# Splitting a stage's third weight block among the normalised highs, and moving the stages' SBUF region ahead of the small tiles

## The reference

```python
def rms_norm(x, g):
    y = xf * lax.rsqrt(jnp.mean(xf * xf, axis=-1, keepdims=True) + RMS_EPS)
    return (y * g).astype(x.dtype)
u = modulate(rms_norm(h, norm2_g[l]), sh2, sc2)
h = h + g2 * (relu(u @ w1) ** 2 @ w2)
```

## Time and profile before

| | us |
|---|---|
| median of 3 runs | 2047.86 |
| the runs | 2047.71, 2047.86, 2052.12 |
| profiled execution, its time | 2051.87 |
| profiled execution, its span | 2050.1 |
| busy in the span: PE | 1994.9 |
| DVE | 960.3 |
| ACT | 682.7 |
| POOL | 914.1 |
| mean granted TensorE clock | 0.983 of full speed |

### The profile page before, as it was taken

One profiled execution on the slowest core, in us unless ns is written; L12 is line 12 of the kernel. 1 busy time (PEld: TensorE's weight loads), 2 busy tenths in 40 slices (PEclk: granted clock), 3 DMA queues, 4 the chain that ended last, 5 costly groups with the idle time before them and its releaser, 6 DMA issues. The chain is left out here.

```text
span 2050.1 us, 25693 instructions
## 1 busy us (share of the span) xinstructions
PE 1994.9 (97%) x10116; PEld 1634.1 (80%) x10116; DVE 960.3 (47%) x1471; ACT 682.7 (33%) x900; POOL 914.1 (45%) x699
## 2 busy tenths in 40 slices
PE   8998998999999999999998999999999999999998
PEld 6875787888888888888887767888888887888887
DVE  4477858583937451413233264266663453113123
ACT  4231733121212431222233354355654342122122
POOL 3323364454545524545454212444344554444444
PEclk9998999999999999999999999999999999999999
DMA  8535132443523312222222111221222222222221
GB/s 349 179 93 213 43 144 109 179 177 147 209 82 148 136 63 99 86 102 95 89 102 89 62 42 59 101 83 62 83 73 92 83 83 103 85 101 103 84 81 42
DMA packets 42783, 223.07 MB, mean 109 GB/s; under 512 B 12737, under 2 KB 13249, under 8 KB 17345
## 3 DMA queue, kind: packets, MB, share of 16 engines
q1 hardware_dynamic: 42688, 221.77, 29.5%
HBM read 217.55 MB, written 2.10 MB: 107 GB/s over the span
## 5 line engine op out<-in xcount | busy, mean ns | idle before, releaser
L970 POOL TENSOR_TENSOR wl<-raw,wh 128x512 fp32r<-128x512 f32 x611 | 833.5, 1395 | 1048.7 <-ACT wh L528 976.3
L1076 PE MATMUL bank<-uh,wh 128*128 128x512 f32 x1432 | 573.9, 401 | 18.4 <-POOL wl L970 17.3
L1078 PE MATMUL bank<-uh,wl 128*128 128x512 f32 x1432 | 560.9, 392 | 0.0
L1077 PE MATMUL bank<-ul,wh 128*128 128x512 f32 x1432 | 560.6, 392 | 0.0
L528 ACT ACTIVATE wh<-raw 128x2048 fp32r<-128x2048 f32 (+1 forms) x152 | 287.0, 1888 | 590.1 <-PE bank L1078 585.6
L1076 PEld LDWEIGHTS bank<-uh,wh 128*128 128x128 f32 x1432 | 270.8, 189 | 87.3 <-POOL wl L970 19.0
L1076 PE MATMUL bank<-ah,wh 128*128 128x512 f32 x848 | 336.2, 396 | 0.0
L1078 PE MATMUL bank<-ah,wl 128*128 128x512 f32 x848 | 334.8, 395 | 0.0
L1077 PE MATMUL bank<-al,wh 128*128 128x512 f32 x848 | 334.7, 395 | 0.0
L1077 PEld LDWEIGHTS bank<-ul,wh 128*128 128x128 f32 x1432 | 270.9, 189 | 57.5 <-issue 3.6
L1078 PEld LDWEIGHTS bank<-uh,wl 128*128 128x128 f32 x1432 | 270.5, 189 | 57.4
(11 more groups left out here) (265 smaller groups left out, 2125.6 us busy)
## 6 DMA issues: line engine op xcount, KB each, us to landing
raw<-in_w SPq DMA_DIRECT2D x64, 1024.0 KB, 5.0
mraw<-in_w_modr SPq DMA_DIRECT2D x32, 1024.0 KB, 4.8
raw<-in_w_gu SPq DMA_DIRECT2D x22, 1024.0 KB, 4.8
raw<-in_w_hg SPq DMA_DIRECT2D x16, 1024.0 KB, 4.9
raw<-in_w_in SPq DMA_DIRECT2D x8, 1024.0 KB, 10.5
modf<-in_w_modf SPq DMA_DIRECT2D x8, 1024.0 KB, 19.7
raw<-in_w_out SPq DMA_DIRECT2D x8, 1024.0 KB, 5.6
mmid<-in_w_modr SPq DMA_DIRECT2D x8, 1024.0 KB, 4.8
```

Of the source, the lines that this page charges most:

```text
L970: last = pool.tensor_tensor(wl[:, b % 2, k:k + 2], raw[:, b % RAW, k:k + 2], f32(wh[:, b % 2, k:k + 2]), ALU.subtract)
L1076: pe.matmul(out, ah_, bh, start=first, stop=False)
L1077: pe.matmul(out, ah_, bl, start=False, stop=False)
L1078: return pe.matmul(out, al_, bh, start=False, stop=last)
```

## The change

Two things. The split of block b0 + 2 of the stages mlp0, mix2 and ffn is made in two halves of four chunks, ahead of the normalised highs k = 4 and k = 5. The first half (`part=0`) waits for the load of the block and for TensorE's end with block b0; the second (`part=1`, L517) counts the semaphore up. The split behind the first block's own work is left out in its place. And the region A of the stages stands directly behind wl, at offset 112 KB = 114688; the small tiles follow behind its 92 KB.

```diff
+THIRD = {"mlp0": FIRST["mlp0"] + 2, "mix2": FIRST["aq"] + 2, "ffn": FIRST["ffn"] + 2}
...
         wl = at("wl", [P, 2, KC, BC], F32R, o); o += 16 * KB
+        A = o
+        o += 92 * KB
         con = at("con", [P, C_END + 3], F32, o); o += 1568
...
         rc = at("rc", [P, 2, 4], F32, o); o += 32
-        A = (o + 31) // 32 * 32
...
                         split(beside, part=k - 2)
                     if between is not None and k == 6:
                         between()
+                    if name in EARLY and k in (4, 5):
+                        split(THIRD[name], part=k - 4)
                     act.wait_ge(t_ready, 8 * i + k + 1)
...
-                        if not last or j < 7:
+                        if (not last or j < 7) and not (first and j == 0):
                             split(b0 + j + 2, q, 8)
...
-                split(b0 + j + 2)
+                if j:
+                    split(b0 + j + 2)
```

## The result

| | before, us | after, us |
|---|---|---|
| median of 4 runs | 2049.99 | 2021.34 |
| lowest and highest | 2047.71, 2052.40 | 2020.06, 2024.76 |
| profiled execution, span | 2050.1 | 2019.8 |

The ratio is 0.9859, 95% interval 0.9844 to 0.9875: 1.4% faster, 28.7 us between the medians; 31.5 were forecast, and a median of 2016.4 within 2008 to 2037. (A fourth run of before has moved its median from 2047.86 to 2049.99.) In a later comparison on one chip, five runs of each or more, the changed kernel had 2022.01 against 2053.08, ratio 0.9843 (0.9825 to 0.9861).

A forecast was written before the change was run, and what follows sets the result against it. TensorE, busy 1994.9 of 2050.1 us, was taken as the bound, through its standstills and its pass pace. Gains of 14.8 (early split) and 16.7 us (region's move), 31.5 together, took the median 2047.86 to 2016.4 us, range 2008 to 2037.

The forecast's parts named there:

- The three stalls and their clock price: TensorE's third-block waits in mlp0, mix2, ffn plus slow passes after: 22.2 us together, 6.6 in mix2, 7.0 in ffn.
- ScalarE's cover: ScalarE's two 1.05 us split copies fit its idle time between normalised highs; cost taken as 0.
- GpSimd beside the lows: GpSimd's subtractions beside VectorE's last three lows end the norm 0 to 2.6 us later, 1.8 taken; TensorE still in time.
- Block four of mlp0: Its load waits behind VectorE's first modulation sum; TensorE stands 5.3 us until 350.0, leaving mlp0 a gain of 1.2 us.
- The region's move: Region A to 114688: 2592 passes on ah, al, mh, ml go from 233.3 to 226.7 ns, 16.7 us taken.
- the place within 16 KB: Candidate cause of slow passes on region A: its tiles' place within 16 KB; if so, the move gains 16.7 us.
- lying beyond the weights: Other candidate cause of slow passes on region A: its lying beyond the weights; if so, the move gains 0.
- The sum: Whole kernel: 14.8 + 16.7 = 31.5 us off the median 2047.86, giving 2016.4 us.
- part 1: Third block's split made early in mlp0, mix2 and ffn: 1.2 + 13.6 = 14.8 us gained.
- part 2: Region A moved in front of the small tiles, aligned to 16 KB: 16.7 us gained.
- waits that only move: Rival: early split only moves waits, each stage gives 1 to 3 us; 2025 or 2042 us; chance 0.10.
- the move does nothing: Rival: moving region A gains nothing, as the cost comes from lying beyond the weights; 2033.1 us; chance 0.33.

The follow-up runs named there:

- early_load: Changed kernel with each of mlp0's modulation loads behind the next weight block's load in SP's queue; median 2018.79 us against before's 2055.43, ratio 0.9838.

## Why the prediction came out right, step by step

The mechanism held in both parts, with three steps mis-sized or misread: the ground for the move, its worth in mlp0, and how a low is held up by GpSimd.

- **The three stalls and their clock price**: 22.2 us to be had, by the trace. In mix2 and ffn they went whole, 6.79 and 7.21 against 6.6 and 7.0 forecast.
- **ScalarE's cover**: right. Two copies of 1.04 and 1.05 us, and the last two highs wait for VectorE as before.
- **GpSimd beside the lows**: 1.8 us of delay forecast for the norm, 1.4 measured; TensorE never waited for a low in the second block. The forecast's other ends, nothing and 2.6, would both have been worse. The single lows were not at 1.2 to 1.6 us as forecast, but at 1.00, 1.00 and 1.77. The Trainium skill (SBUF, State Buffer, section on the two separate sides) says that of a GpSimd operation that reads SBUF and a VectorE one with two SBUF inputs the one that starts second fully blocks. The trace agrees: each lengthened operation ends 0.54 to 0.56 us after the subtraction that it met. The forecast refused the rule because it took it to cost a whole subtraction for each low, 3.8 us; what is waited out is only the rest of one that has begun, here 0.25, 0.25 and 1.02 us.
- **Block four of mlp0**: the step that mattered most for the shape of the result. Naming the chain (modulation sum, load, split, low half) before the run gave a wait of 5.3 us and a start at 350.0; 5.29 and 349.9 were measured, and early_load confirmed the chain. The start of the block came 3.2 us earlier (3.1 forecast), the clock's fall then cost 1.6 us and not 2.0; the net gain was 1.70 against 1.2.
- **The region's move**: the sign was right and the size nearly, 15.3 against 16.7 us. The term was mis-sized in mlp0: there most stretches on ah went from 233.2 to 228.2 ns a pass, 5.0 and not 6.6, and 768 passes x 1.6 ns are 1.2 us. Both means hold one pause of 0.32 us at the loop's turn; without it the passes took 232.3 ns in before, where mlp1's took 233.3, and 227.2 in after. Why the loss was smaller there isn't known. The reason was only half right. I had set the place within 16 KB against lying beyond the weights. The second is refuted, since the region still lies beyond them; of the first only the last 8 bits of the address count, and only against the weights' address. That the forecast was right all the same is partly luck: a place at a multiple of 16 KB is one at a multiple of 256 bytes too.
- **The sum**: 15.7 + 15.3 = 31.0 against 31.5 forecast. It came closer than its terms did, as part 1 gave 0.9 us more and part 2 1.4 less. That the medians show 28.7, and on another chip 31.1, is within what the first 46 us and the clock's falls scatter.
- **The rivals**: waits that only move happened in one stage of three, as was in the sum already. That the move does nothing had 0.33; the rows had nothing more to decide it. The Trainium skill (TensorE: Matmul & The Clock Gate, back-to-back issue gap) spoke for it, as its formula has no term for the operand's place. The page calls it the gap of an isolated matmul; for these passes, each with a weight load, neither its 216 ns nor a single value came out: the runs show 226.7, 229.0 (a mean) and 233.3 ns for passes that differ in place alone.

## What to carry to other kernels

When the same matmul has two paces in one trace, compare start to start over a long stretch (the listed duration hides most of it), and look at how the streamed and the weight tile lie to each other in SBUF as well as at the other engines. When a stall is cut, follow the next block's whole chain, queue by queue: in two stages it had slack, in the third it ended 5.3 us late on a load that stood behind another engine's work. And where an engine is busy throughout such a stretch, as VectorE is at the start of mlp0, putting its work in another order moved the wait rather than removing it, here in two tries.

## What the runs showed of the hardware that I had not expected

A pass of 512 columns in fp32r takes 226.7 ns from start to start when the streamed tile and the weight tile have the same address within 256 bytes, and 233.3 when they are 128 bytes apart in it, whichever of the two is moved; shifting both changes nothing. At 64 bytes (only the streamed tile was moved) the mean is 229.0, from 225.9 to 231.7 by kind of pass. A VectorE operation of 128x512 with two SBUF inputs that GpSimd lengthens ends 0.54 to 0.56 us after GpSimd's operation, in all 133 cases of one trace. And two executions of one kernel differed by 3.6 us at the start of mlp0, 3.5 of them from the first 46 us.
